# In the hybrid mixer of a three-mixer transformer kernel: the place of the zero fills, of the weight splits and of the output scaling in the engines' orders

## The reference, cut to what matters

```python
proj = h @ w_in          # 2052 columns: q_a k_a v_a x_b g_b q_c k_c v_c f_c
y_a = sliding_window_sink_attention(q_a, k_a, v_a, sinks)     # 8 heads, 2 key/value heads
y_b = rg_lru(causal_depthwise_conv_2(x_b)) * gelu(g_b)        # 256 channels
y_c = forgetting_attention(q_c, k_c, v_c, log_sigmoid(f_c + fox_bf))   # 4 heads
y = concatenate([rms_normalize(y_a), rms_normalize(y_b), rms_normalize(y_c)]) * out_gain
return y @ w_out
```

## Time and profile before

| | us |
|---|---|
| median of 3 runs | 2861.96 (2858.73 to 2862.71) |
| the profiled execution's own time | 2862.71 |
| its span in the profile | 2861.5 |
| TensorE busy | 2698.6 (94%) |
| VectorE busy | 1636.8 (57%) |
| ScalarE busy | 727.3 (25%) |
| GpSimd busy | 797.1 (28%) |

### The profile page before, as it was taken

One profiled execution on the slowest core, in us unless ns is written; L12 is line 12 of the kernel. 1 busy time (PEld: TensorE's weight loads), 2 busy tenths in 40 slices (PEclk: granted clock), 3 DMA queues, 4 the chain that ended last, 5 costly groups with the idle time before them and its releaser, 6 DMA issues. The chain is left out here.

```text
span 2861.5 us, 32762 instructions
## 1 busy us (share of the span) xinstructions
PE 2698.6 (94%) x12810; PEld 2192.0 (77%) x12810; DVE 1636.8 (57%) x2381; ACT 727.3 (25%) x1335; POOL 797.1 (28%) x796
## 2 busy tenths in 40 slices
PE   6999999999999999999999999999999899769994
PEld 5888887777778888888888799888888678656673
DVE  4343468888755545555455556553334567646766
ACT  2101125555521101111011245421001145322332
POOL 1111121112111111121111268621111310025775
PEclk9999999999999999999999999999999999969997
DMA  3333332222224434445344400033333362137895
GB/s 105 96 96 96 96 95 69 67 73 64 62 74 133 140 111 147 125 126 147 111 142 130 145 15 1 1 96 96 96 96 96 68 86 40 32 140 272 316 338 198
DMA packets 439323, 317.35 MB, mean 111 GB/s; under 512 B 33841, under 2 KB 403842, under 8 KB 438914
## 3 DMA queue, kind: packets, MB, share of 16 engines
q1 hardware_dynamic: 417048, 274.31, 33.1%
q10 hardware_dynamic: 15498, 32.54, 3.6%
q0 software_dynamic: 6624, 8.41, 0.9%
HBM read 314.67 MB, written 16.25 MB: 116 GB/s over the span
## 5 line engine op out<-in xcount | busy, mean ns | idle before, releaser
L225 POOL TENSOR_SCALAR w_hi<-w_lo_exact 128x1024 fp32r<-128x1024 f32 x369 | 413.3, 1120 | 1826.0 <-DMA w_lo_exact<-in_ffn_w_gate 409.2
L240 PE MATMUL bank<-h_hi,w_hi 128*128 128x512 f32 x1992 | 792.2, 398 | 23.0 <-DVE h_lo L312 11.0
L241 PE MATMUL bank<-h_lo,w_hi 128*128 128x512 f32 x1992 | 779.9, 392 | 0.0
L242 PE MATMUL bank<-h_hi,w_lo 128*128 128x512 f32 x1992 | 779.9, 392 | 0.0
L232 DVE TENSOR_TENSOR w_lo<-w_lo_exact,w_hi 128x1024 fp32r<-128x1024 f32 x369 | 454.8, 1234 | 138.9 <-POOL w_hi L225 138.0
L240 PEld LDWEIGHTS bank<-h_hi,w_hi 128*128 128x128 f32 x1992 | 376.9, 189 | 109.8 <-issue 19.4
L241 PEld LDWEIGHTS bank<-h_lo,w_hi 128*128 128x128 f32 x1992 | 377.1, 189 | 79.3 <-issue 3.4
L242 PEld LDWEIGHTS bank<-h_hi,w_lo 128*128 128x128 f32 x1992 | 376.7, 189 | 79.7
L240 PE MATMUL bank<-g_hi,w_hi 128*128 128x512 f32 x704 | 278.4, 396 | 0.0
L241 PE MATMUL bank<-g_lo,w_hi 128*128 128x512 f32 x704 | 278.4, 396 | 0.0
L242 PE MATMUL bank<-g_hi,w_lo 128*128 128x512 f32 x704 | 278.4, 396 | 0.0
(11 more groups left out here) (485 smaller groups left out, 3802.1 us busy)
## 6 DMA issues: line engine op xcount, KB each, us to landing
w_lo_exact<-in_ffn_w_gate SPq DMA_DIRECT2D x88, 512.0 KB, 3.8
w_lo_exact<-in_ffn_w_up SPq DMA_DIRECT2D x88, 512.0 KB, 3.9
w_lo_exact<-in_ssm_w_in SPq DMA_DIRECT2D x48, 512.0 KB, 3.9
mod_w<-in_w_mod ACTq DMA_DIRECT2D x48, 512.0 KB, 3.8
e_lo_exact<-in_w_gate SPq DMA_DIRECT2D x46, 512.0 KB
e_lo_exact<-in_w_up SPq DMA_DIRECT2D x46, 512.0 KB, 9.2
e_lo_exact<-in_w_down SPq DMA_DIRECT2D x46, 512.0 KB, 5.8
w_lo_exact<-in_ffn_w_down SPq DMA_DIRECT2D x32, 512.0 KB, 3.7
```

Source lines behind the costliest of these rows:

```text
L225: ge.tensor_scalar(k.w_hi[:, u % SLOTS, :], k.raw[:, u % SLOTS, :], 1.0, 0.0, ALU.mult, ALU.add).then_inc(*k.up("w hi", u))
L240: te.matmul(k.bank[bank][:, :], hi, x_hi, start=first, stop=False)
L241: te.matmul(k.bank[bank][:, :], hi, x_lo, start=False, stop=False)
L242: return te.matmul(k.bank[bank][:, :], lo, x_hi, start=False, stop=stop)
```

## The change

GpSimd's splits of units 2, 3 and 4 stand ahead of the ten fills, the others behind them as before. VectorE's split of unit n+2 stands behind step n-10 instead of ahead of it, from unit 10 on. The root and scaling of y_b come one head later (after step 10), y_a's squares and sums are ahead of them (after step 9). In the scaling of every part the low part of tile m-1 is made behind the scaling of tile m.

```diff
@@ mixer_pool
+    split_pool(k, u0 + 2, u0 + 5)
     for t in (k.key_hi, k.key_lo):
         fill_pool(k, t[:, :, :, :].rearrange("p a b (c d) -> p (a b c) d", d=P), 0.0, "zeros set")
...
             fill_pool(k, k.vals[:, t, half, :, 1, :], 0.0, "zeros set")
-    split_pool(k, u0 + 2, k.unit_at["moe"] + 2)
+    split_pool(k, u0 + 5, k.unit_at["moe"] + 2)
@@ mixer_scalar
         if s == 9:
+            y_squares_scalar(k, "y a")
+        if s == 10:
             y_hi_scalar(k, "y b")
-            y_squares_scalar(k, "y a")
@@ mixer_vector
-        if n != FIRST_STEP - 1:
+        if n < FIRST_STEP - 1:
             split_vector(k, u0 + n + 2)
...
             mixer_bias_vector(k, 0)
-            split_vector(k, u0 + n + 2)
         if n >= FIRST_STEP:
             mixer_step_vector(k, n - FIRST_STEP)
+        if n >= FIRST_STEP - 1:
+            split_vector(k, u0 + n + 2)
...
         if s == 9:
+            y_sums_vector(k, "y a")
+        if s == 10:
             y_scale_vector(k, "y b")
-            y_sums_vector(k, "y a")
@@ y_scale_vector
     for m in range(k0, k0 + n):
-        t = k.nht[:, m % 2, :]
         ve.wait_ge(*k.last("y lo"))
-        ve.scalar_tensor_tensor(t, k.y[m], ...).then_inc(*k.up("y scaled", m))
-        ve.wait_ge(*k.at("y hi", m))
-        ve.tensor_tensor(k.y_lo[:, m, :], t, ..., ALU.subtract).then_inc(*k.up("y lo", m))
+        ve.scalar_tensor_tensor(k.nht[:, m % 2, :], k.y[m], ...).then_inc(*k.up("y scaled", m))
+        if m > k0:
+            y_lo_vector(k, m - 1)
+    y_lo_vector(k, k0 + n - 1)
+
+def y_lo_vector(k, m):
+    k.ve.wait_ge(*k.at("y hi", m))
+    k.ve.tensor_tensor(k.y_lo[:, m, :], k.nht[:, m % 2, :], ..., ALU.subtract).then_inc(*k.up("y lo", m))
```

More of the change, by code:

```diff
@@ L2440, in y_scale_vector @@
     for m in range(k0, k0 + n):
-        t = k.nht[:, m % 2, :]
         ve.wait_ge(*k.last("y lo"))
-        ve.scalar_tensor_tensor(t, k.y[m], k.col("out_gain", m), k.nr[:, :], ALU.mult, ALU.mult).then_inc(*k.up("y scaled", m))
-        ve.wait_ge(*k.at("y hi", m))
-        ve.tensor_tensor(k.y_lo[:, m, :], t, k.y_hi[:, m, :].bitcast(F32), ALU.subtract).then_inc(*k.up("y lo", m))
+        ve.scalar_tensor_tensor(k.nht[:, m % 2, :], k.y[m], k.col("out_gain", m), k.nr[:, :], ALU.mult, ALU.mult).then_inc(*k.up("y scaled", m))
+        if m > k0:
[3 more added lines that the diff above has]
+    k.ve.wait_ge(*k.at("y hi", m))
+    k.ve.tensor_tensor(k.y_lo[:, m, :], k.nht[:, m % 2, :], k.y_hi[:, m, :].bitcast(F32), ALU.subtract).then_inc(*k.up("y lo", m))
 EXTRAS_AT = [3 * n + 2 for n in range(EXTRA)]
```

## The result

| | before | after |
|---|---|---|
| median of 10 runs, us | 2858.61 (2853.48 to 2863.47) | 2865.69 (2862.56 to 2871.91) |
| ratio | | 1.0022 [1.0012, 1.0032] |
| profiled execution, us (span) | 2862.71 (2861.5) | 2862.56 (2861.3) |

The changed kernel is slower by 7.1 us in the medians, 0.22% by the ratio, with 3.4 to 9.1 us in its interval. The two profiled executions are equally long all the same. In the one after, the stages ahead of the mixer took 3.0 us more, and what lies behind it 6.6 less, though the two programs are the same in both places. So I compare the mixer by itself.

A forecast was written before the change was run, and what follows sets the result against it. TensorE, busy 94% of the span, was taken as the bound, so its idle or half-clock time counts. 14.5 - 2.7 - 4.6 - 4.4 = 2.8 over 2862.71 us gave 2865.5, stated as 2865; range 2856 to 2871.

The forecast's parts named there:

- within 0.2%: Whole kernel: time not told from no change, 2856.2 to 2867.7 us; chance 0.63, against faster 0.11 and slower 0.26.
- fills and normalisation: Mixer's start: the fills' loss of 14.5 us and the normalisation's gain of 2.7 leave TensorE 11.8 late after unit 4.
- steps: Mixer steps: VectorE's splits behind the steps let step 7's row maxima start sooner, a gain of 4.6 us.
- tail: y's tail: pipelined scaling and y_b's scaling one head later, a gain of 4.4 us.
- Part 1b: Unit 4: ten fills after its late load hold VectorE's cast and split, TensorE idles 13 us; a loss of 14.5.
- Part 1a: Normalisation at the mixer's start: without fills beside VectorE's first scalings, TensorE starts sooner, a gain of 2.7 us.
- Part 2: Steps 0 to 7: splits behind the steps start the maxima 6.6 us sooner at step 0, 4.6 at step 7.
- the other splits cost nothing there: Steps up to 7: TensorE's 9.5 us cover VectorE's list of 8.6 to 9.5; without cover each split costs 1.23.
- The rival that VectorE takes the whole gain: Steps 1 to 7: VectorE becomes the bound and the moved splits give nothing; price 4.6 us, 2870; chance 0.15.
- Part 3: y's tail: 1.0 us for y_b's scaling one head later, 3.4 for y_a and y_c pipelined; a gain of 4.4.
- the hold does not bind: Fills: they end before VectorE needs them, so only the gains stay, 2851 us; chance 0.08.
- Three whole splits hold VectorE's restart: Behind the fills: GpSimd's three splits each hold VectorE's small operations whole, 2.1 us more, 2867.6; chance 0.15.

The follow-up runs named there:

- exp. 1: Kernel before with only the ten GpSimd fills moved behind the split of unit 4; 2871.97 us, 1.0039.
- exp. 2: Kernel before with only VectorE's splits of unit n+2 moved behind the steps; 2858.85 us, 0.9988.
- exp. 3: Kernel before with only the tail changed: y_b's root and scaling behind step 10, y_a's squares and sums ahead, scaling pipelined; 2857.77 us, 0.9986.
- exp. 8: Kernel before with the pipelined scaling alone, y_b's scaling left behind step 9; 2859.53 us, 0.9994.
- 9: Kernel before with only y_b's root and scaling moved behind step 10, y_a's squares and sums ahead of them, not pipelined; 2862.43 us, 1.0001.
- experiment 7: Changed kernel with the ten fills done twice in their place, VectorE waiting for the second set; 2876.29 us, 1.0056.
- experiment 6: Changed kernel with the csp_both and selector fills first under their own count, the eight others behind GpSimd's split of unit 8; 2853.56 us, 0.9971.
- 10: Kernel of experiment 6 with y_b's scaling left behind step 9; 2850.82 us, 0.9963.
- experiment 5: Changed kernel with the ten fills one unit earlier, between GpSimd's splits of units 3 and 4; 2858.25 us, 0.9991.
- experiment 4: Changed kernel with VectorE's split of unit 4 ahead of the cast that waits for the zeros; 2862.75 us, 1.0005.

## Why the prediction was right, and where its terms were off

The time (2865.0, measured 2865.69) and the range held, and so did the mechanism. That the time is met to 0.7 us is luck: I had 3 us over a base of 2861.96, and the base came out 3.4 lower and the difference 4.1 larger, at 7.1. The likeliest case of the three chances was "within 0.2%"; the ratio is 1.0022, just on the slower side. The mixer alone gives 3.4, which is the lower end of the interval. What is above that isn't in the two traces, and I leave it open; the last section shows one thing that moves executions by this much.

| term, us | forecast | by itself | in the changed kernel |
|---|---|---|---|
| fills and normalisation | +11.8 | +9.9 (exp. 1, step 0) | +9.9 |
| steps | -4.6 | -2.9 (exp. 2, step 7) | -2.7 |
| tail | -4.4 | -2.9 (exp. 3), -4.6 (exp. 8) | -3.9 |
| sum | +2.8 | | +3.4 |

The last column: TensorE's units 9 to 11, ahead of the steps, start 9.9 later; step 7 is 7.2 later (2.7 won by then, 6.2 at step 0 and 3.5 of it lost again), the last update 3.4 later (3.9 more). The terms are rounded, the sum is that of the traces.

- **Part 1b held in its chain.** Fills quiet, 8.4 us in all for 8.2; cast to split 5.42 us for 5.27; the idle time 13.50 for 13; unit 4 later by 8.2 for 9.25. The half clock behind it was shorter than its term: the matmuls run at 0.427 us each from 2312.09 to 2315.6, 3.5 us where I had taken 5.3 from the start of the mixer. That is 8 matmuls at 0.2, 1.6 and not 2.5.
- **Part 1a was too small**, 2.7 for 3.8: unit 3's split fell behind the first two scalings and not on them (2274.01), so the 0.5 for it was not owed, and the first scaling itself began 0.55 sooner (relative 3.3 for 3.8), which I had left where it was the earlier trace rows. The latter is the channel sum ahead of it, whose two matmuls took 1.12 us for 1.67. It would have brought nothing before: in experiment 2, with the fills unmoved, the first scaling starts at 3.3 too and the first h matmul still at 9.5. By these 1.1 and the 0.9 of the half clock the forecast's 11.8 becomes 9.8, where experiment 1 shows 9.9 at step 0.
- **Part 2's gain at step 0 was about right** (6.2 for 6.6), its remainder wrong: 2.7 for 4.6. The failing step is "the other splits cost nothing there": the moved splits go with a loss of 1.8 at step 2, and of 1.7 at step 7, where the split comes between VectorE's weights and its next maxima. For 7 I had counted one split, 1.23. Of the 0.8 at step 3 it isn't shown that the splits cause it. The rival that VectorE takes the whole gain was half right.
- **Part 3's size was about right, its attribution not.** I gave the move 1.0 and the pipelining 3.4. Together they gave 3.9 in the changed kernel. The low parts of y_a's tiles follow each other every 1.39 us, where I had 1.47 and before has 2.17. Experiments 8 and 9 give the pipelining all of it and the move nothing. I had seen that TensorE would stand some 3.8 us at step 11 (it stood 4.06) and still counted a gain.
- **The rival "the hold does not bind"** fell with the wait of 11.38 us and with experiment 7.
- **Three whole splits hold VectorE's restart**: the three small operations took 1.19 + 1.40 + 1.08 us for 0.41 + 0.68 + 0.35 in a kernel where they are undisturbed (0.42, 0.68 and 0.35 in experiment 6), and GpSimd's splits 3.66 together. So 2.2 us were lost there, where the forecast had 0.76 + 1.05 = 1.8 and the rival 3.15. VectorE was held, but its own 1.44 us run inside the time of the splits, and cast to split came out at 5.42 and not 6.6.

## What to carry to other kernels

A wait on a semaphore that counts several things makes its reader wait for the last of them. Before work is put behind another in an engine's list, look who waits for each piece, give the piece that is needed first a count of its own, and put the rest where nobody waits (9 to 11 us here, against a loss of 7). An idle stretch counts as a hole only up to the load that ends it, and only where the work doesn't hold another engine up: behind the load of unit 4 the fills cost 9.9 us net at step 0, and ahead of it, beside the normalisation, they set unit 4 back by 6.1 against experiment 6. And moving a block of VectorE's work from one head's chain to the next only changed which wait it showed up as here; making the block shorter is what gained.

## What the runs showed of the hardware

**The clock comes back at different times in executions with the same work.** After a wait of 2.2 us at y's last tiles, the changed kernel and kernel 6 run the same instructions. TensorE's timeline of the changed kernel (its first line, 2486.05, stands in the first section) and of kernel 6:

```profile
2487.13 0.63 PE L240 MATMUL bank<-y_hi,w_hi 128*128 128x512 f32 x1
```

```profile
2474.27 0.50 PE L240 MATMUL bank<-y_hi,w_hi 128*128 128x512 f32 x1 [2.25 <-DVE y_lo L2454]
...
2475.08 0.40 PE L240 MATMUL bank<-y_hi,w_hi 128*128 128x512 f32 x1
```

One is at the lower level (1.2 GHz, a matmul each 0.43 us) for about 3 us, the other at full clock (2.4 GHz, each 0.23). From there to the update of x they differ by 1.5 us. The difference is larger behind the mixer. Windows of 10 us that start 12.2 us behind the last update of x, before and then after, the program being the same there:

```profile
2529.70:2539.70 10.00, 10.00 (x40) 9.13 (x39) 3.52 (x6) 3.41 (x6) 0.00 (x0) 0.50 0.62 247
```

```profile
2536.07:2546.07 10.00, 10.00 (x64) 9.14 (x64) 3.64 (x6) 3.42 (x6) 1.69 (x2) 0.92 0.61 248
```

TensorE is busy throughout in both and gets through 40 matmuls in one and 64 in the other. Both begin at the lower level 7.2 us behind the last update. Before stays there for 21.5 us of work without a gap (2524.70 to 2546.2), after for 6.5 (2531.07 to 2537.6). So the router's logits are transposed 30.3 us behind the last update before and 23.3 after, which is 7.0, and all of the 6.6 us behind the mixer. Of the 13 traces three run like before (before itself, experiments 8 and 10: 30.2 to 30.3), the others at 21.9 to 24.8, with one program behind the mixer in all. Why the clock stays low in some isn't shown. Differences of a few microseconds between single profiled executions are therefore nothing to reason from unless the granted clock of both is read beside them.

**GpSimd's long operations held VectorE's for their whole length.** In experiment 5 the two operations of VectorE beside the two key fills take 3.22 and 3.23 us, and the fills 3.18 each, where 0.75 and 2.75 are their quiet times. In experiment 4 a split took 3.76 for 1.22 beside a key fill. The Trainium skill (SBUF - State Buffer, Who interferes with whom) calls the port pair that both share an exclusive lock held for a whole instruction; these traces agree. They show besides that GpSimd's own operation grows in the encounter, by 0.4 each in experiment 5 and by 1.0 for the second key fill of experiment 4 (3.72), and that in the changed kernel three splits end to end cost VectorE 2.2 us and not 3.15, as its own operations ran within their time.
